# Swapping rows for the rotary embedding: a product with a permutation matrix, or four small transfers

## The reference, cut to what matters

```python
HEAD_DIM = 64
ROPE_DIM = HEAD_DIM // 4
ROPE_THETA = 500000.0

def _partial_rope(x, cos, sin):
    half = ROPE_DIM // 2
    x1 = x[..., :half]
    x2 = x[..., half:ROPE_DIM]
    rot = jnp.concatenate([x1 * c - x2 * s, x2 * c + x1 * s], axis=-1)
    return jnp.concatenate([rot, x[..., ROPE_DIM:]], axis=-1)

def _token_mixing(h, ...):      # of the second block, called once a layer
    z = h @ w_in                # 1024 -> 6000 columns or so, cut into parts
    ... three attentions: dq, dk (dilated, 6 heads), q, k_sel, k_win are roped
    merged = g_a * (y_a @ br_nsa) + g_b * (y_b @ br_dil) + g_c * (y_c @ br_fox)
    return merged @ w_out
```

## Time and profile before

| | us |
|---|---|
| median of 3 runs | 2423.36 (2421.65 to 2424.78) |
| the profiled execution's own time | 2421.88 |
| its span in the trace | 2420.1 |
| TensorE busy | 2388.7 |
| VectorE busy | 1651.3 |
| ScalarE busy | 1208.5 |
| GpSimd busy | 233.8 |
| TensorE's granted clock, share of full | 0.999 |

### The profile page before, as it was taken

How to read it: one execution, slowest core, us unless ns; L and a number is a source line. 1 busy time by engine, 2 the same in 40 slices (tenths; PEclk the granted TensorE clock), 3 DMA queues, 4 the chain that set the end, 5 groups by cost and what they waited for, 6 DMA issues and landing times. The chain is left out here.

```text
span 2420.1 us, 39354 instructions
## 1 busy us (share of the span) xinstructions
PE 2388.7 (99%) x16673; PEld 2178.4 (90%) x16673; DVE 1651.3 (68%) x2158; ACT 1208.5 (50%) x1448; POOL 233.8 (10%) x334
## 2 busy tenths in 40 slices
PE   8999999999999999999999999999999999999998
PEld 6998998898899999799889899889988989988997
DVE  4786877787786697788678665575555556557554
ACT  5445565434434556444443456944444445694443
POOL 2000003000200000300110001210001000121000
PEclk9999999999999999999999999999999999999999
DMA  8895556797887564689589665456656655545653
GB/s 280 296 309 168 175 164 220 258 305 234 290 299 242 161 183 158 229 290 304 180 302 306 206 170 150 131 184 209 201 183 205 189 176 170 153 130 190 212 183 114
DMA packets 371551, 514.59 MB, mean 213 GB/s; under 512 B 23712, under 2 KB 312726, under 8 KB 371376
## 3 DMA queue, kind: packets, MB, share of 16 engines
q1 hardware_dynamic: 344976, 415.80, 53.5%
q0 software_dynamic: 26400, 96.28, 11.7%
HBM read 510.89 MB, written 1.13 MB: 212 GB/s over the span
## 5 line engine op out<-in xcount | busy, mean ns | idle before, releaser
L1141 DVE TENSOR_TENSOR lo<-raw,hi 128x2048 fp32r<-128x2048 f32 x382 | 876.7, 2297 | 436.4 <-ACT hi L743 435.4
L743 ACT ACTIVATE hi<-raw 128x2048 fp32r<-128x2048 f32 (+2 forms) x393 | 749.3, 1910 | 475.7 <-PE ps L1780 206.2
L1780 PE MATMUL ps<-NH,hi 128*128 128x256 f32 x3360 | 951.2, 283 | 0.0
L1780 PE MATMUL ps<-NL,hi 128*128 128x256 f32 x3360 | 942.1, 280 | 0.0
L1780 PE MATMUL ps<-NH,lo 128*128 128x256 f32 x3360 | 940.5, 280 | 0.0
L1780 PEld LDWEIGHTS ps<-NH,hi 128*128 128x128 f32 x3360 | 632.4, 188 | 13.5 <-issue 10.1
L1780 PEld LDWEIGHTS ps<-NL,hi 128*128 128x128 f32 x3360 | 633.2, 188 | 3.1
L1780 PEld LDWEIGHTS ps<-NH,lo 128*128 128x128 f32 x3360 | 634.1, 189 | 0.0
L1780 PE MATMUL ps<-hi,NH 128*128 128x512 f32 (+4 forms) x768 | 280.5, 365 | 12.4 <-DVE lo L1141 6.6
L1780 PE MATMUL ps<-hi,BH 128*128 128x512 f32 (+1 forms) x768 | 291.6, 383 | 0.0
L1780 PE MATMUL ps<-hi,BL 128*128 128x512 f32 (+1 forms) x768 | 288.6, 379 | 0.0
(11 more groups left out here) (316 smaller groups left out, 1997.2 us busy)
## 6 DMA issues: line engine op xcount, KB each, us to landing
raw<-in_ffn_w_in SPq DMA_DIRECT2D x176, 512.0 KB, 4.9
raw<-in_ffn_w_gu SPq DMA_DIRECT2D x174, 512.0 KB, 5.7
arena<-in_ada_w POOLq DMA_DIRECT2D x72, 1024.0 KB, 6.3
raw<-in_w_in SPq DMA_DIRECT2D x92, 512.0 KB, 4.6
raw<-in_ffn_w_down SPq DMA_DIRECT2D x88, 512.0 KB, 4.4
raw<-in_ffn_w_out SPq DMA_DIRECT2D x88, 512.0 KB, 4.4
raw<-in_mix_w_in SPq DMA_DIRECT2D x86, 512.0 KB, 4.6
raw<-in_w_branch SPq DMA_DIRECT2D x16, 512.0 KB, 4.1
```

The costliest lines, as they stand in the source:

```text
L743: last = nc.scalar.activation(dst, src, ACT.Copy)
L1141: last = nc.vector.tensor_tensor(dst, src, part.bitcast(F32), ALU.subtract)
L1780: last = nc.tensor.matmul(dst, a, b, start=start and k == 0, stop=stop and k == 2, skip_group_check=skip)
```

## The change

The two products with the permutation matrix go, and with them the matrix, its load and TensorE's two waits. In their place GpSimd issues four transfers for each roped unit, from Z to RT[:, 1], 8 partitions of 2 x 256 elements each (16 KB): rows 8 to 15 go to rows 0 to 7, rows 0 to 7 to rows 8 to 15, and the same for rows 64 to 79. They are issued after `ev r` and, from the second on, after the rope of the unit before it. VectorE waits for the semaphore of all four, and multiplies RT[:, 1] by the sines in place. The minus is now in the table of sines. The rows that aren't turned are set to zero once at the start of each mixer by GpSimd, since their sine is zero and what stands there must be finite.

```diff
-                                             (SWAP, i["swap"]), (DUP.rearrange("p a b -> p (a b)"), i["dup"]),
+                                             (DUP.rearrange("p a b -> p (a b)"), i["dup"]),
...
+        def swap_target(l, u):
+            return 16 * 4 * (len(ROPED) * l + ROPED.index(u) + 1)
...
             def mix(s):                                  # GpSimd
                 norm_tile(s.before, 1)
                 m.stage = s.key
+                if s.block == 2:
+                    pool.wait_ge(dve_done, at("dve", "n 1 1", s.before))
+                    nc.gpsimd.memset(RT[:, 1], 0.0).then_inc(pool_done, done("pool", "rope pads"))
+                    pool.wait_ge(pool_done, at("pool", "rope pads"))
                 for u in range(OUT1):
                     for work in side_work(s, u):
+                        if work[:4] == "rope":
+                            r = int(work[4:])
+                            pool.wait_ge(act_done, at("act", f"ev {r}"))
+                            if r != ROPED[0]:
+                                pool.wait_ge(dve_done, at("dve", f"rope {ROPED[ROPED.index(r) - 1]}"))
+                            for base in (0, 8, 64, 72):
+                                src = base ^ 8
+                                pool.dma_start(RT[base:base + 8, 1], Z[src:src + 8, r % 2]).then_inc(swap_in, 16)
...
                 if work[:4] == "rope":                   # VectorE
                     u = int(work[4:])
-                    dve.wait_ge(pe_done, at("pe", f"swap {u}"))
+                    dve.wait_ge(swap_in, swap_target(int(m.stage[1]), u))
                     nc.vector.tensor_tensor(RT[:, 0], Z[:, u % 2], spread(ROPE[:, 0, :], 1, 2), ALU.mult)
-                    nc.vector.tensor_tensor(RT[:, 1], ps[:, 5, :].rearrange("p (a t) -> p a t", a=2), spread(ROPE[:, 1, :], 1, 2), ALU.mult)\
+                    nc.vector.tensor_tensor(RT[:, 1], RT[:, 1], spread(ROPE[:, 1, :], 1, 2), ALU.mult)\
...
-                if work[:4] == "rope":                   # TensorE
-                    u = int(work[4:])
-                    pe.wait_ge(act_done, at("act", f"ev {u}"))
-                    if u != ROPED[0]:
-                        pe.wait_ge(dve_done, at("dve", f"rope {ROPED[ROPED.index(u) - 1]}"))
-                    for k in range(2):
-                        last = nc.tensor.matmul(ps[:, 5, T * k:T * k + T], SWAP, Z[:, u % 2, k, :], start=True, stop=True)
-                    last.then_inc(pe_done, done("pe", f"swap {u}"))
...
-            sin[base + r] = sin[base + 8 + r] = np.sin(ang[r])
-            swap[base + 8 + r, base + r] = -1
-            swap[base + r, base + 8 + r] = 1
+            sin[base + r], sin[base + 8 + r] = -np.sin(ang[r]), np.sin(ang[r])
```

More of the change, by code:

```diff
@@ L295, in program @@
         ROPE = place("block2", 2, T)
-        SWAP = place("block2", P)
         DUP = place("block2", 2, P)
@@ L338, in program @@
         vrow_in = sem("vrow_in")
+        swap_in = sem("swap_in")
         rows_out = sem("rows_out")
@@ L344, in program @@
         pe_done, act_done, dve_done, pool_done = sem("pe_done"), sem("act_done"), sem("dve_done"), sem("pool_done")
-        EARLY_CONSTS, CONSTS, SMALL1, SMALL2, CONSTS2 = 4, 3, 6, 4, 6
+        EARLY_CONSTS, CONSTS, SMALL1, SMALL2, CONSTS2 = 4, 3, 6, 4, 5
         VROWS1, VROWS2 = 5, 3
@@ L2153, in side2 @@
                 what, _, g = work.partition(" ")
-                if work[:4] == "rope":
-                    u = int(work[4:])
-                    pe.wait_ge(act_done, at("act", f"ev {u}"))
-                    if u != ROPED[0]:
-                        pe.wait_ge(dve_done, at("dve", f"rope {ROPED[ROPED.index(u) - 1]}"))
-                    for k in range(2):
-                        last = nc.tensor.matmul(ps[:, 5, T * k:T * k + T], SWAP, Z[:, u % 2, k, :], start=True, stop=True)
-                    last.then_inc(pe_done, done("pe", f"swap {u}"))
-                elif work == "dup":
+                if work == "dup":
                     pe.wait_ge(dve_done, at("dve", f"rope {KV_U}"))
@@ L2345, in constants @@
     cos, sin = np.ones((P, T), f), np.zeros((P, T), f)
-    swap = np.zeros((P, P), f)
     for base in (0, 64):
@@ L2349, in constants @@
             cos[base + r] = cos[base + 8 + r] = np.cos(ang[r])
-            sin[base + r] = sin[base + 8 + r] = np.sin(ang[r])
-            swap[base + 8 + r, base + r] = -1
-            swap[base + r, base + 8 + r] = 1
-    c["rope"], c["swap"] = np.concatenate([cos, sin], 1), swap
+            sin[base + r], sin[base + 8 + r] = -np.sin(ang[r]), np.sin(ang[r])
+    c["rope"] = np.concatenate([cos, sin], 1)
     half = np.eye(64, dtype=f)
```

## The result

The changed kernel takes 2437.16 us (median of 4 runs, 2434.04 to 2439.89) against 2422.51 (4 runs, 2421.2 to 2424.78) of the kernel before on the same chip. The ratio is 1.006, 95% interval 1.0048 to 1.0072: slower by 14.6 us, where 2425 and at most 2435 were forecast. The profiled execution is the fastest of the four, 2434.04 with a span of 2432.2, 12.1 us above the span of before.

The account below looks back on a forecast made before the run. TensorE, busy 99%, bounds the kernel; it saves 9.2 us but spends them waiting for ropes, `qk d2` coming 0.8 us later, 1.5 in both mixers: 2423.4 profiled, median 2425, range 2417 to 2435.

Parts of the forecast that it names:

- What goes: On TensorE in two mixers: 10 swaps and a wait vanish, saving 4.6 us a mixer, 9.2 us in all.
- The change of place: TensorE would wait 1 to 4 us at `qk d0` for VectorE's rope, less at `dup`, `qk d1`, `qk d2`.
- median time to landing: Rope transfers, last issue to landing: called the deciding number; forecast wrong if below 2.2 or above 4.6 us.
- Which L: Time from a rope's last transfer issue to its landing: taken as 3.3 us, halfway between 2.8 and 3.8.
- two branches: Start of `qk d2`: 1452.34 plus four landing times by the rope chain, or 1457.1 plus two by TensorE's own chain.
- (b): Rival at `qk d0` and later waits: transfers meet weight loads each time, landing 4 to 5.3 us; 2434.5 to 2441; chance 0.34.
- The hand-over: Between VectorE and GpSimd, and landing and VectorE: two hand-overs per rope, together about 0.15 us.
- The granted clock: TensorE from `qk d0` to `qk d2`: taken as 14.2 us, as before; no fall of the clock was forecast.
- The late end: End of the program: the prediction had no term for it; behind `qk d2` nothing should change.
- (a): Rival on the rope transfers: quick landing in 1.8 to 2.5 us, gain stays, 2416.5 to 2418.5 us; chance 0.28.
- (c): Rival at rope 5's issues: VectorE's six copies hold up GpSimd, 1.3 us a mixer, 2.6 in all, 2427.5; chance 0.08.
- (d): Rival behind VectorE's new wait: split weights come late, needing landing above 7 us; 0.02 of (b)'s chance.

Follow-up runs that it names:

- e1: Changed kernel with the four transfers of each unit left out, so keys and queries aren't turned: 2412.92 us, ratio 0.9961 to the kernel before.
- e4: Changed kernel with SyncE holding the loads of units 11 to 14 until ropes 5 to 8 are done: 2449.18 us, ratio 1.0116 to before.
- e9: Changed kernel with 66 products of zeroes on TensorE ahead of `qk d0`: 2433.33 us, ratio 1.0049 to the kernel before.
- e5: Changed kernel with the loads of units 12 and 13 reading another weight in 4 KB instead of 512-byte rows: 2431.83 us, ratio 1.0041 to before.
- e6: Changed kernel with two buffers for swapped rows and ScalarE issuing the transfers instead of GpSimd: 2417.4 us, ratio 0.9982 to the kernel before.
- e10: Changed kernel with two buffers for swapped rows and SyncE issuing the transfers instead of GpSimd: 2413.83 us, ratio 0.9964 to the kernel before.
- e2: Changed kernel with two buffers for swapped rows, so transfers wait only for their unit's copy: 2417.99 us, ratio 0.9983 to the kernel before.
- e3: Changed kernel with 48 products of zeroes on TensorE ahead of `qk d0`: 2432.88 us, ratio 1.0043 to the kernel before.

## Why the prediction was wrong, point by point

**What goes: right.** 9.2 us was forecast, e1 gives 9.08.

**The change of place: right in kind.** The step it names, a wait at `qk d0` for VectorE's rope, is there; four issues take 2.0 us (2.2 forecast); VectorE waits for DMA from T to T at ropes 5 to 8. But the wait is 7.6 and 6.6 us where 1 to 4 were forecast, and the smaller ones at `dup`, `qk d1` and `qk d2` aren't there. The median time to landing, which the prediction called the number that decides, was 2.8 and 2.5 us, inside the 2.2 to 4.6 in which it held itself right; it didn't decide. Ahead of the first mixer nothing moved (`ev 4` 0.3 us early).

**The step that failed: "Which L", one value for all ropes.** The mean of the four was 3.3 us in either mixer, just what I took. But it is not spread evenly: ropes 5 and 6 had 2.8 + 6.5 and 5.1 + 4.2, so 9.3 us together in either mixer in place of 6.6, ropes 7 and 8 1.8 to 2.3 each. The formula has two branches, 1452.34 + 4L for `qk d2` behind all ropes and 1457.1 + 2L behind rope 6 only. With one L of 3.3 the first decides (1465.5). With the true values the second does, since it takes only those of ropes 5 and 6: 1457.1 + 9.3 = 1466.4. I had even written that each unit's end starts a load and that a meeting is the rule, and gave that to rival (b) as a larger L, instead of asking which rope meets a load. That the ropes behind a wait are quick is part of the same mechanism: TensorE, waiting, frees no slot, and no load starts. e4 and e9 show it by undoing it. By itself this is 0.9 us a mixer; it also set the length of TensorE's wait.

**Three terms that were missing or too small**, all on the path, and more than four fifths of the miss:
- The hand-over from the rope's end to GpSimd's issue is 0.56 us, not the 0.15 of TensorE's, from which I took it; less 0.1 for the quicker issues it is 0.3 a rope, 0.6 to rope 6. An engine's hand-over was read from another engine's row.
- The granted clock, the largest: the prediction took 14.2 us from `qk d0` to `qk d2`, as at full clock, and they took 16.34 and 16.85. Of that 2.05 and 2.55 us are the clock's, behind waits of 7.6 and 6.6 us; behind e5's wait of 3.6, the length that one L of 3.3 gives (1449.5 against 1445.9), it was still 1.5. I had not asked what an idle TensorE costs beyond the idle time.
- The late end, 3.3 us, which the prediction put at nothing; no trace of it is in the profile of before.

The sum for the first mixer: 1466.4 + 0.6 + 2.05 - 0.3 (the early start) = 1468.8, where `qk d2` started at 1468.83. For the whole, the profiled execution took 2434.04 us where the prediction's sum for it is 2423.4, 10.6 less: 1.8 by the uneven L, 1.2 by the hand-overs, 4.6 by the clock and 3.3 by the end, less 0.3 for the early start, make 10.6.

**The rivals.** (b) was right in its place, `qk d0` (1452.0 forecast for L = 4.5, 1452.49 measured), and in half of its reason: two ropes of four met a load, and the waits that it put behind `qk d0` aren't there. That its 2434.5 to 2441 holds the result is in part luck, since 4.6 us of the clock and 3.3 of the end, which it doesn't have, are in it. (a) is out: quick transfers of 1.8 us exist, as the Trainium skill's "DMA: Bandwidth & Descriptors", section "Anatomy of one DMA", has it (about 2.0 us and little for 16 KB), but only without a load beside them; with one the same 16 KB took up to 7.7 us. (c) is out: GpSimd issued rope 5's transfers from 1435.61, in the midst of the six copies, and they took 2.03 us against 1.99 elsewhere. VectorE's row:

```profile
1435.16 1.30 DVE L1613 COPY arena<-arena 128x256 f32<-128x256 f32 x6
```

(d) did not occur: TensorE waits at most 0.4 or 0.5 us for a split, as before.

**What is open.** Why the end is late with many transfers by GpSimd; why e6's median isn't lower; and why the four runs of the changed kernel lie between 2434 and 2440. That a transfer meets a load by chance of some 0.1 us would do it (e9's rope 8), but no run shows it.

## What to carry to other kernels

A small transfer that stands in a chain with the work is not to be priced by its size, nor by a mean: look for each one separately at what the DMA engines do in the microseconds in which it is issued; here it was 2 us alone and 3 to 8 beside a load. A wait that it puts on TensorE costs more than its length: 1.5 to 2.55 us more here, by the clock, behind waits of 3.6 to 7.6 us. If it can't be made early, give it a second buffer, so that it waits for its source only; this took the loss of 14.6 us to a gain of 4. Then choose the issuer that has nothing else to do: the same transfers were worth another 4 us when SyncE issued them in place of GpSimd.

## What the runs showed of the hardware that I had not expected

- Four transfers of 16 KB issued by GpSimd were usable 1.8 to 2.3 us after the last issue with idle DMA engines, and after 2.8 to 7.7 us beside a 1 MB load. The double buffer doesn't make them quicker (7.6 and 7.7 us to landing at the longest).
- Forty small transfers by GpSimd made the program end 3.3 us later; twenty 0.9; ten 0.1. The same transfers by ScalarE or SyncE did not (3.9 and 4.2 us against 3.9). The Trainium skill, in "DMA: Bandwidth & Descriptors", section "SWDGE vs HWDGE vs iDMA", says that a plain transfer belongs on SyncE or ScalarE. For SyncE the runs agree, by 4.2 us between e10 and e2; for ScalarE they show no gain (e6 against e2), since it had other work to do.
- The granted clock fell while TensorE was idle and stayed at half for 6.8 us in the first mixer and 10.2 in the second, most of it beside work. Behind shorter idle stretches (3.6 us in e5, 2.1 in e3) it fell only after the work had begun again, 0.9 and 1.4 us into it. With 66 small products of zeroes, 3.86 us, in the wait it stayed up (e9), with 48 it did not (e3).
- GpSimd started an issue 0.56 us after VectorE's rope was done, TensorE a product 0.06 us after (1450.42 + 2.01 = 1452.43 to 1452.49).
